# Transfers from SyncE, splits in another order, first maxima between groups, a result sent tile by tile: a hybrid decoder trunk on one core

## The reference

```
x = x + 0.5 * swiglu(rms_norm(x, ffn1_norm), ffn1_w_gate, ffn1_w_up, ffn1_w_down)   # width 2816
x = x + hybrid_mixer(rms_norm(x, mix_norm), ...)
x = x + 0.5 * swiglu(rms_norm(x, ffn2_norm), ffn2_w_gate, ffn2_w_up, ffn2_w_down)
```

```
tb = t.reshape(B, S // 16, 16, G, D)                    # compression of k and v
blocks = concatenate([tb[:, :-1], tb[:, 1:]], 2) + pe   # 31 blocks of 32 positions
kc, vc = gelu(flat @ w1) @ w2, for k and for v
p_c = masked_softmax(q . kc)                            # compressed branch
p_s, p_w = masked_softmax(q . k_slc), masked_softmax(q . k_win)   # exact row maxima
o = g0 * (p_c @ vc) + g1 * (p_s @ v_slc) + g2 * (p_w @ v_win)
```

## Time and profile before

| | |
|---|---|
| runs | 2841.6, 2852.1, 2856.66 us |
| median | 2852.1 us |
| the profiled execution's own time | 2845.81 us |
| its span in the trace | 2844.0 us |
| PE busy | 2714.7 us, 95% of the span |
| DVE, ACT, POOL busy | 1259.6, 1013.8, 1073.8 us |
| mean granted TensorE clock | 0.990 |

### The profile page before, as it was taken

The page is one execution under the profiler, slowest core; times in us unless marked ns, Lnnn a source line. Parts: engine busy times, 40 slices in busy tenths (PEclk is TensorE's granted clock), DMA queues, the critical chain, the costliest instruction groups (busy, mean ns, idle before and its releaser), DMA issues.

```text
span 2844.0 us, 37156 instructions
## 1 busy us (share of the span) xinstructions
PE 2714.7 (95%) x13268; PEld 2162.2 (76%) x13268; DVE 1259.6 (44%) x1596; ACT 1013.8 (36%) x1487; POOL 1073.8 (38%) x450
## 2 busy tenths in 40 slices
PE   7999999999998899999999999999999888999998
PEld 5888887766776787888878888877667667878887
DVE  6333353466446365332353323444563562643322
ACT  4222233545545433222242222344555454332211
POOL 3444444421222344444434444443113223444443
PEclk9999999999999999999999999999999999999999
DMA  3222223201211122223222232232111112232221
GB/s 137 90 102 105 102 74 111 104 31 38 68 56 45 67 100 94 103 88 117 89 77 100 92 111 96 88 107 80 45 34 62 61 45 73 98 103 94 102 108 70
DMA packets 36070, 239.54 MB, mean 84 GB/s; under 512 B 3952, under 2 KB 5232, under 8 KB 13936
## 3 DMA queue, kind: packets, MB, share of 16 engines
q1 hardware_dynamic: 32720, 232.80, 23.1%
q10 hardware_dynamic: 3232, 5.17, 0.5%
HBM read 234.81 MB, written 2.10 MB: 83 GB/s over the span
## 4 chain that ended last, share of the span: by engine, by line
issue 62%; POOL 25%; PE 11%; POOLq 1%; DMA 0%; DVE 0%; ACTq 0%; ACT 0%; DVEq 0%
POOL wlo L272 25%; PE bank L1194 4%; PE bank L1196 4%; PE bank L1195 4%; POOLq L271 1%; POOLq L267 1%; DMA x<-xT 0%; DVE hlo L693 0%; DVE x L763 0%; DVE hhi L691 0%; POOLq L272 0%; POOL vcm L256 0%; POOL selr L257 0%; ACTq L281 0%; ACT L278 0%
## 5 line engine op out<-in xcount | busy, mean ns | idle before, releaser
L272 POOL TENSOR_TENSOR wlo<-raw,whi 128x1024 fp32r<-128x1024 f32 (+2 forms) x440 | 1072.3, 2438 | 1751.0 <-ACT whi L304 863.5
L1194 PE MATMUL bank<-hhi,whi 128*128 128x512 f32 x1984 | 797.2, 402 | 30.4 <-POOL wlo L272 28.7
L1196 PE MATMUL bank<-hhi,wlo 128*128 128x512 f32 x1984 | 777.3, 392 | 0.0
L1195 PE MATMUL bank<-hlo,whi 128*128 128x512 f32 x1984 | 776.3, 391 | 0.0
L295 ACT ACTIVATE whi<-raw 128x1024 fp32r<-128x1024 f32 (+1 forms) x232 | 264.0, 1138 | 714.8 <-PE bank L1196 714.8
L1194 PEld LDWEIGHTS bank<-hhi,whi 128*128 128x128 f32 x1984 | 376.0, 190 | 118.7 <-issue 36.5
L1196 PEld LDWEIGHTS bank<-hhi,wlo 128*128 128x128 f32 x1984 | 374.7, 189 | 79.2
L1195 PEld LDWEIGHTS bank<-hlo,whi 128*128 128x128 f32 x1984 | 375.4, 189 | 75.7 <-issue 3.4
L750 DVE TENSOR_TENSOR tmp<-tmp,bank 128x512 f32<-128x512 f32 x80 | 55.0, 688 | 534.2 <-PE bank L1196 534.2
L304 ACT ACTIVATE whi<-raw 128x1024 fp32r<-128x1024 f32 (+2 forms) x176 | 173.8, 988 | 296.2 <-PE bank L1196 145.9
L1194 PE MATMUL bank<-uhi,whi 128*128 128x512 f32 x704 | 274.4, 390 | 0.0
(11 more groups left out here) (281 smaller groups left out, 3096.9 us busy)
## 6 DMA issues: line engine op xcount, KB each, us to landing
raw<-gu SPq DMA_DIRECT2D x88, 1024.0 KB, 4.7
raw<-dn SPq DMA_DIRECT2D x32, 1408.0 KB, 6.0
raw<-cb SPq DMA_DIRECT2D x48, 768.0 KB, 4.2
raw<-pM SPq DMA_DIRECT2D x16, 1024.0 KB, 4.8
raw<-cq SPq DMA_DIRECT2D x16, 1024.0 KB, 4.8
raw<-pA SPq DMA_DIRECT2D x12, 1024.0 KB, 4.8
raw<-wo SPq DMA_DIRECT2D x8, 1024.0 KB, 4.8
x<-xT ACTq DMA_DIRECT2D x4, 512.0 KB, 7.2
```

The lines of the kernel that those rows point to most:

```text
L272: pool.tensor_tensor(wlo[:, s, 0:w], raw[:, j, lo:lo + w], whi[:, s, 0:w].bitcast(f32), ALU.subtract).then_inc(sem["lo_done"], 1)
L1194: mm(outp, wh, mhi, start=start and k == 0, stop=False)
L1195: mm(outp, wh, mlo, start=False, stop=False)
L1196: i = mm(outp, wl, mhi, start=False, stop=stop and k == len(parts) - 1)
```

## The change

Seven edits:

- The eight transfers `zde` to `ee` are issued by SP, ahead of the loads of `cq`, behind a wait for `zde_ready`. ACT neither waits for `zde` nor issues them.
- ACT splits tiles 2 and 3 of `pM0` first, then rounds k's blocks, splits `cq` 0, rounds v's blocks, splits `cq` 1.
- PE waits for `xlo` of k ahead of k's tiles, and for that of v ahead of v's.
- DVE finds the maxima of step 0 between group 0 and group 1.
- PE waits for ACT's copies of the compressed probabilities behind `scores(1)` instead of ahead of it.
- In a step of the attention ACT does all copies and exponentials, and the splits that are due behind them.
- In `gu0` the matmul of the sum stands behind k = 7 instead of k = 3. The result is sent in eight transfers of 256 KB, each when its tile of x is ready.

```diff
+                    if name == "cq":
+                        sp.wait_ge(sem["zde_ready"], me.at("zde_ready", 2))
+                        for kv in range(2):
+                            for par2 in range(2):
+                                for g in range(2):
+                                    sp.dma_start(ee[par2 * HD:(par2 + 1) * HD, kv, g], zde[g * HD:(g + 1) * HD, kv, par2]
+                                                 ).then_inc(sem["ee_ready"], 16)
...
-            sp.wait_ge(sem["unit_free"], L * UNITS + credit["unit_free"])
-            sp.dma_start(out.rearrange("(k p) t -> p k t", p=P), x[:]).then_inc(sem["x_out"], 16)
-            sp.wait_ge(sem["x_out"], 16)
+            for c in range(KD):
+                sp.wait_ge(sem["unit_free"], L * UNITS - KD + c + 1 + credit["unit_free"])
+                sp.dma_start(out[c * P:(c + 1) * P], x[:, c]).then_inc(sem["x_out"], 16)
+            sp.wait_ge(sem["x_out"], 16 * KD)
...
-                act.wait_ge(sem["zde_ready"], me.next("zde_ready", 2))
                 act.wait_ge(sem["con_in"], 48)
-                for kv in range(2):
-                    for par2 in range(2):
-                        for g in range(2):
-                            act.dma_start(ee[...], zde[...]).then_inc(sem["ee_ready"], 16)
                 split_tile("pM0", 2)
+                split_tile("pM0", 3)
                 act.wait_ge(sem["xf_ready"], me.next("xf_ready", 4))
                 A(xhi[:, xcols(0, 0, 16)], ...)
-                split_tile("pM0", 3)
+                split_tile("cq", 0)
                 act.wait_ge(sem["xf_ready"], me.next("xf_ready", 4))
                 A(xhi[:, xcols(1, 0, 16)], ...)
-                split_tile("cq", 0)
                 split_tile("cq", 1)
...
                         if m + 1 < NPAIR * NB:
                             exps(m + 1, q)
+                    for q in range(4):
                         fill("pM1", PM1, 4 + 4 * m + q)
...
                 for g in range(2):
                     pg = pc[:, g, :, 0:NCMP]
+                    if g:
+                        maxima(0, 0)
+                        maxima(0, 1)
...
-                maxima(0, 0)
-                maxima(0, 1)
                 for m in range(NPAIR * NB):
...
-                        if k == (3, 0, 1)[f]:
+                        if k == (7, 0, 1)[f]:
...
                 section("pM0", hp, hp)
-                pe.wait_ge(sem["xlo_ready"], me.next("xlo_ready", 2))
...
                     kv, half = i // 2, i % 2
+                    if half == 0:
+                        pe.wait_ge(sem["xlo_ready"], me.next("xlo_ready"))
...
-                pe.wait_ge(sem["cs_pt"], me.next("cs_pt", 2))
                 def values(m):
...
+                    if m == 0:
+                        pe.wait_ge(sem["cs_pt"], me.next("cs_pt", 2))
                     for q in range(4):
                         pe.wait_ge(sem["s_p"], me.next("s_p"))
```

More of the change, by code:

```diff
@@ L240, in _ @@
                     wide = w.shape[-1]
+                    if name == "cq":
+                        sp.wait_ge(sem["zde_ready"], me.at("zde_ready", 2))
+                        sp.sem_inc(sem["held"], 1)
+                        for kv in range(2):
[3 more added lines that the diff above has]
+                                                 ).then_inc(sem["ee_ready"], 16)
                     with sp.Fori(0, n // 2) as i:
@@ L425, in gate_unit @@
                     return after
-                act.wait_ge(sem["zde_ready"], me.next("zde_ready", 2))
                 act.wait_ge(sem["con_in"], 48)
-                for kv in range(2):
-                    for par2 in range(2):
-                        for g in range(2):
-                            act.dma_start(ee[par2 * HD:(par2 + 1) * HD, kv, g], zde[g * HD:(g + 1) * HD, kv, par2]
-                                          ).then_inc(sem["ee_ready"], 16)
                 split_tile("pM0", 2)
+                split_tile("pM0", 3)
                 act.wait_ge(sem["xf_ready"], me.next("xf_ready", 4))
                 A(xhi[:, xcols(0, 0, 16)], xf[:].rearrange("p l g c -> p (l g c)"), ACT.Copy).then_inc(sem["xhi_ready"], 1)
-                split_tile("pM0", 3)
+                split_tile("cq", 0)
                 act.wait_ge(sem["xf_ready"], me.next("xf_ready", 4))
                 A(xhi[:, xcols(1, 0, 16)], xf[:].rearrange("p l g c -> p (l g c)"), ACT.Copy).then_inc(sem["xhi_ready"], 1)
-                split_tile("cq", 0)
                 split_tile("cq", 1)
@@ L920, in _, with maxima @@
                     dve.wait_ge(sem["cs_sub"], me.next("cs_sub"))
+                def maxima(m, w):
+                    dve.wait_ge(sem["s_mm"], me.next("s_mm", 2))
+                    dve.tensor_reduce(st2[:, m % 2, 0, 2 * w:2 * w + 2], banks[:, 2 + 2 * w:4 + 2 * w, 0:(m % NB + 1) * P],
+                                      AX.X, ALU.max, negate=True).then_inc(sem["s_max"], 1)
                 for g in range(2):
                     pg = pc[:, g, :, 0:NCMP]
+                    if g:
+                        maxima(0, 0)
+                        maxima(0, 1)
                     dve.wait_ge(sem["cs_exp"], me.next("cs_exp"))
@@ L936, in _ @@
                 fill_group(3)
[L938 to L942, removed]
                 def nsa_parts(tt):
```

## The result

The changed kernel takes 2826.7 us (median of 4 runs, 2823.3 to 2828.1), the kernel before 2850.8 (4 runs, 2841.6 to 2856.7). The ratio is 0.9912, with a 95% interval of 0.9894 to 0.9931: faster by 0.9%, some 25 us. The forecast was 2825 in a range of 2811 to 2843.

What follows compares the result with a forecast made beforehand. PE, busy 95% of the span, bounds the kernel. Terms 6.1 + 2.4 + 5.0 + 6.5 + 4.1 = 24.1 us give 2821.7 from the profiled execution or 2828.0 from the median; forecast 2825, range 2811 to 2843.

Steps and rivals of the forecast that it cites:

- Compression: Compression: PE's waits at tiles 2 and 3 of pM0 go, 3.1 us a layer, 6.1 in all, between 4.5 and 6.5.
- The two waits become one of 2.3 us: At cq in the compression: PE's next two waits, 1.03 and 0.92 us, merge into one; no gain counted.
- The rival of a late load: Compression: SP's load of cq comes too late and gives the 6.1 us back, 2831; chance 0.04.
- Norm: Norm of gu0: the sum's matmul behind k = 7 saves 1.2 us a layer, 2.4 in all, between 0.5 and 4.
- the chain from the sum to "the seventh tile": gu0: a chain through ACT and DVE to the seventh tile's split; PE can only save what it saves.
- a rival at the seventh tile: gu0: longer idleness ahead of the seventh tile drops PE's clock, costing 5.4 us in both layers, 2831; chance 0.12.
- Handover: Handover to the attention: PE's wait of 2.49 us a layer goes, 5.0 us in all, 3.5 if maxima cost 0.75 each layer.
- Second layer only: Handover: PE's wait for group 1, 1.8 us, occurs in the second layer only and stays.
- Splits at a step's end: Attention steps: moving splits behind copies and exponentials saves 6.5 of the 7.3 us waited for prt, between 3 and 7.3.
- The deduction for POOL holding DVE: Attention steps: POOL's moved work may hold DVE's scaling up to 2.5 us, so 6.5 of 7.3 us was taken.
- Result: End of kernel: the last 256 KB lands in 3.0 us instead of 7.1, saving 4.1 us, between 3.1 and 4.5.
- New waits: Steps, handover and norm: new waits replace the old, leaving 14 us gained, 2838 to 2840; chance 0.17.

## Why the prediction was right, step by step

**What bounds it.** Right. The busy time of PE fell by 1.8 us, the span by 22.6. The waits named went, and the parts add up.

**Compression (6.1, traces 5.2).** The mechanism is right in each step but one: no wait at tiles 2 and 3, transfers and load of SP in the forecast interval and hidden. "The two waits become one of 2.3 us" was not: they became two of 1.69 and 1.62, because DVE frees bank 0 behind v's blocks, which the forecast did not look at, and because the split of `cq` 1 stood behind the rounding of v, which it gave only as the lower bound. The order alone gave 0.9 a layer at most and nothing in the runs; it needed the transfers off ACT. The rival of a late load fell: the split of `cq` 0 (469.34) follows the rounding of k without a wait.

**Norm (2.4, traces 0.7, runs 0).** Here a step failed: that the chain from the sum to "the seventh tile" alone sets what PE can save. PE is held earlier. With the sum late it waits for POOL at once (1.39 us) and for `hlo` at the fifth tile (1.98 and 0.53), and in both layers of this trace it reaches the seventh so late that nothing is left to wait for there. In five of the eight passes with the late sum (a pass is one layer in one trace; four kernels have the late sum) the seventh tile has its wait too, of 1.69 to 2.15 us. The forecast worked in the second layer and doubled. But in the first layer of the kernel before, PE waits for `hlo` at the fifth tile already, where the second has no wait, and 2.20 us at the seventh instead of 1.33 (timeline of PE):

```profile
50.52 0.50 PE L1194 MATMUL bank<-hhi,whi 128*128 128x512 f32 x1 [0.50 <-DVE hlo L717]
```

The chain gained nothing either. Ln did start early, 1.28 us after the start of the sum instead of 2.11, but that is not the edit's doing: with the sum behind k = 3 its matmuls ran at full clock (1.12 to 1.22 us) in 13 of 20 passes, and of the ten second layers among them only that of the trace before had the 2.07 us that the forecast read. DVE then lost it again: `fs` took 9.69 us for eight instructions, with two of POOL's subtractions beside them (1434.27 and 1438.75), against 7.53 in the trace before. I had expected POOL's moved work to free `hlo`; it met `fs` as well. From the start of the sum to the end of `hlo` it took 21.8 to 21.9 us in seven of the eight passes with the late sum, and 21.4 to 21.8 in 17 of the 20 with k = 3, against 20.3 in the pass that the forecast read. And the fall of the clock, which I had as a rival at the seventh tile, came at the fifth. It took the place of the old one. Against the second layer of the changed kernel with k = 3 it was longer (two of the six windows below 1.00 instead of one), and so took back what the shorter waits had saved.

**Handover (5.0, traces 6.5, alone 7.4 by the ratio).** The waits went as forecast. What I did not see is the clock. These are stretches of 12 us, chosen by me, from PE's first transposes of the compressed probabilities, in the kernel before (both layers):

```profile
576.00:588.00 12.00, 8.86 (x61) 5.96 (x61) 8.24 (x18) 6.25 (x23) 2.39 (x1) 1.00 0.05 9
1985.00:1997.00 12.00, 9.17 (x53) 6.22 (x55) 5.42 (x16) 6.25 (x23) 2.39 (x1) 0.86 0.04 5
```

in the kernel with ACT's order alone (first layer):

```profile
572.00:584.00 12.00, 7.74 (x33) 5.23 (x32) 6.44 (x16) 5.46 (x20) 2.75 (x2) 0.72 0.00 1
```

and in the changed kernel (first layer):

```profile
570.00:582.00 12.00, 10.23 (x71) 7.03 (x69) 8.40 (x23) 6.46 (x24) 3.71 (x2) 1.00 0.00 1
```

In the six traces with the old handover (these two, the steps, the norm, the compression and the result alone) the clock was under 1.00 in 7 of 12 such windows, between 0.72 and 0.86. In the eight with one or both of the handover edits it was 1.00 in all 16. So the edits save, besides their wait, a fall that each layer had about every second time. It is not the only one at this place. In the 12 us ahead of the transposes, before any edited code of PE, the clock was under 1.00 in 7 of the 12 passes with the old handover and in 13 of the 16 with the new. So it was in the changed kernel's second layer:

```profile
1960.00:1972.00 12.00, 12.00 (x102) 10.03 (x101) 7.93 (x18) 3.69 (x11) 2.71 (x1) 0.86 0.27 89
```

With the old handover the clock fell behind the transposes in all 5 passes that had kept it ahead of them, and in 2 of the 7 others. No run shows whether the edits have a part in the earlier fall. The wait for group 1 goes by it: it was 1.76 or 1.77 us in just the eight passes, of all 28, whose clock had not fallen in those 12 us, and at most 0.57 in the others. "Second layer only" was thus a matter of the clock and not of the layer. The term was mis-sized: 5.0 for the waits, plus 1.1 us in the one layer that fell behind the transposes in the profiled execution of before.

**Splits at a step's end (6.5, traces 8.4).** Right, and more than the whole of the listed waits. The deduction for POOL holding DVE was wrong: in the step shown POOL's subtraction (579.10 to 581.44) falls between DVE's scales. By windows over the 16 steps PE's idle time fell by 7.0 us over both layers together (9.0 to 2.0) and its busy time by 1.5. No wait of PE is left in these steps.

**Result (4.1, traces 5.1, alone 3.4 to 4.7).** Right in kind; the last 256 KB landed in 2.0 us, where I had taken 3.0. The estimate of 2.6 us by the Trainium skill, DMA: Bandwidth & Descriptors, "Anatomy of one DMA — SWDGE (gpsimd) path", lay nearer than the one by my row, though that section gives its fixed part for transfers that GpSimd issues, and these are SP's.

**Rivals.** New waits did take the place of the old at the norm, and in part at `cq`, but not in the attention. No split at a step's end reached PE late.

**Sum.** That 2825 came within 2 us of 2826.7 is in part luck. Terms that were too high (0.9 and 1.7) and too low (1.5, 1.9 and 1.0) offset each other, and the 1.7 us by which the touched sections gave more than forecast were taken back by the untouched ones, in which the profiled execution before was 3.2 us shorter than that after. That is also why it was right to start above the profiled time.

## What to carry to other kernels

When a wait is to be taken away, look for the next thing that the waiting engine needs along each of its paths, a bank to be freed and a split as much as the data, and not only for the one that waits longest now: at the norm and at `cq` it was the second in line that bound. What an engine waits for is paid by what stands behind it in its program: one split moved ahead of ACT's wait made 7 us of difference (2831.1 against 2823.6). A reading of one pass is a thin base for a term: the norm was forecast from the one second layer of ten whose sum ran at half clock. And idle time of PE costs more than itself if the clock falls behind it, so taking a wait at a place where the clock sometimes falls is worth more than the wait, while moving it may bring nothing.

## What the runs showed of the hardware

- The eight transfers of 64 KB within SBUF took 2.0 us each to land from SP ahead of the load, and 4.0 us from ACT beside it. It was 2.0 in each kernel in which SP issued them and the load of 1 MB came behind, and 4.0 to 4.2 in each in which ACT did. Which of the two does it, the issuer or the load behind, no run shows. DVE idled 6.05 us for them instead of 6.79; of the 2.3 us by which it went on earlier than in the kernel before (463.71 against 466.01), 1.6 were lead from earlier sections. Issuing one cost 0.63 us on SP, about as much as on ACT (0.64).
- A transfer of 256 KB from SBUF to HBM landed in 2.0 us with nothing beside it; the median of all eight was 7.1.
- How far a wait brings the clock down is not set by its length alone in these traces: after 2.20 us at `cq`, followed by one of 0.53, it stayed at 1.00, after 2.19 followed by 2.32 it fell to 0.68, and after the 1.98 of the norm, with another 0.53 behind it, it fell to 0.53.
